# Modulation pieces moved between stages, one block-product pair reordered, and the input's fold placed behind the evictions

## The chip, the cores and the metric

The kernel runs on one core of a Trainium2 chip, in one launch. The metric is the device time in microseconds (us), the median of the runs. TensorE (PE) multiplies matrices, VectorE (DVE) and ScalarE (ACT) work elementwise, GpSimd (POOL) and SyncE (SP) here mostly issue DMAs. Each engine runs its own list of instructions in order and waits on semaphores.

## The reference, cut to what matters

One layer over 256 latent tokens (`x`) and 256 context tokens (`ctx`), with 2048 features, all in float32. The nine modulation vectors are `m = silu(c) @ ada_w + ada_b`, each of 2048 values; those for the context come from `c_ctx`.

```python
m_lat = silu(c) @ ada_w + ada_b            # 9 vectors of 2048 for the latent tokens
m_ctx = silu(c_ctx) @ ada_w + ada_b        # the context needs 0 to 4 of them
x   = x   + 0.5 * m_lat[2] * swiglu(modulate(rms_norm(x, g1),   m_lat[0], m_lat[1]), ffn1_w_in, ffn1_w_out)
ctx = ctx + 0.5 * m_ctx[2] * swiglu(modulate(rms_norm(ctx, g1), m_ctx[0], m_ctx[1]), ffn1_w_in, ffn1_w_out)
hx, hc = modulate(rms_norm(x, g2), m_lat[3], m_lat[4]), modulate(rms_norm(ctx, g2), m_ctx[3], m_ctx[4])
x = x + m_lat[5] * (concat(retention(hx, hc), mla(hx, hc)) @ mix_w_out)
x = x + 0.5 * m_lat[8] * swiglu(modulate(rms_norm(x, g3), m_lat[6], m_lat[7]), ffn2_w_in, ffn2_w_out)
return rms_norm(x, final_g)
```

`swiglu(h, w_in, w_out)` is `(silu(h @ gate) * (h @ up)) @ w_out` with 5632 inner features.

## The kernel before

**Products.** Every weight and every activation is split into a high half in fp32r and a low half (the rest), and a product is three matmuls: high by high, low by high and high by low (`three`, L1434 to L1439). A slab of weights lands in `raw`, ScalarE makes its high half `wh` with one copy, VectorE its low half `wl` with one subtraction, and TensorE starts when `wl_ready` counts the slab. Both halves have two slots, so the split of a slab can start only when the slab two before it has been used (`slab_used`). ScalarE and VectorE thus follow TensorE closely, in an order written out by hand in each engine's block.

**Stages of the first half.** 1. A start that makes modulations 0 and 1, the norm and the first three tiles of the gate and up projection. 2. The *standard slabs* (13 tiles, 26 slabs of 48 matmuls with 512 columns, to 458 us). 3. The *pair stage* (28 tiles, `FIRST_S` to `PAIRS`, 458 to 1043 us): the 2x2 block product of latent and context with gate and up halves is done in seven products of half the depth instead of eight, `P1 P5 P6 P3 P7 P2 P4` in this order, each 24 matmuls of 256 columns. They need sums of weight blocks (`w_sum` on VectorE, two accumulating DMAs on GpSimd's queue) and sums of activation blocks, made once (`form`, `last_form`, `form_hi`, `form_lo`). The last of these, the difference that P7 multiplies, overwrites `hh` and `hl`, which the standard slabs still read. P4 adds into a bank that `up_ctx` must have read after P7; `up_ctx` of a tile stands in VectorE's list behind the first low half of the next tile. 4. The *down stage* (44 steps, `STEPS`, 1043 to about 1535 us): step `(part, q, g)` multiplies group `g` of four activation tiles with quarter `q` of the output, four banks `py`, 48 matmuls with 512 columns. Parts are groups 0 to 3, 4 to 7 and 8 to 10. After the last group of a quarter the four banks are evicted: in part 0 by ScalarE (`copy_out`), in parts 1 and 2 by VectorE (`add_out`, L2418 to L2433). The next step's first matmul into a bank waits until its tile has been evicted (`y_free`). A step's iteration on ScalarE and VectorE makes the halves for the step two later (`down_high`, `down_low`). At a quarter 0, `act_high` and `act_low` also split a group of activations. 5. The *mixing stage*: squares and norm of both streams (`hl_tile`), then the slabs of the input projection, in order CQ, RQ, CKV, KR, RK, RV, RG (`S_CQ` and so on; MIX0 is the first), retention and attention. The values' banks are copied to `rv` behind every fourth RV slab. Then the second feed-forward.

**Modulation pieces.** Modulations 2 to 8 are made on VectorE, 14 rounds of 16 *pieces* (`chunk`): a piece is 128 x 1024 of `ada_w`, 512 KB, multiplied by a column of `cs` and added to a sum (`chunk_step`, L2195 to L2197). A single round ("S", modulations 5 to 8, latent only) has one sum `accl`; a double one ("D", 2 to 4) has two, `accl` and `accc`, so its piece costs two instructions. After 16 pieces the sum is reduced over the partitions: `take_turn`, `take_reduce`, `take_total`, for each sum. `STD_CHUNKS`, `S_CHUNKS` and `B_CHUNKS` say how many pieces each slab, pair and step takes. Three buffers hold pieces, and SP issues the load of a piece when the one three before it has been summed (two before it in the double rounds of the standard slabs). Before, rounds lie so: standard slabs S0 S1 D0 D1, pair stage S2 to S7, down stage D2 to D5 in steps 0 to 31.

**The input's fold.** In the down stage the input, which was overwritten, is read again and turned (`xp`, `xq`): SP loads two columns of tiles (`x_piece`), VectorE transposes 32 x 32 blocks into the two banks `two` (`turn(s)`, L2257), ScalarE copies the blocks to their places in `xq` with 16 small copies (`spread(s)`, L922), and VectorE adds (`fold(s)`, L2266). `turn(s)` waits until `spread(s-1)` has emptied the banks, `spread(s)` waits for `turn(s)` and, since `xq` is one buffer, for `fold(s-1)`; eight such rounds cover 16 tiles, from `X_STEP` on. VectorE's loop over the steps, before:

```python
for j in range(len(STEPS)):
    s = j - X_STEP
    ...
    if 1 <= s <= 8:
        fold(s - 1)
    if step_last(j) and STEPS[j][0]:
        add_out(j)
    ...
    if j + 2 < len(STEPS):
        if STEPS[j + 2][1] == 0:
            act_low(STEPS[j + 2][2])
        down_low(j + 2)
    ...
    if -1 <= s < 7:
        turn(s + 1)
```

## Time and profile before

| | |
|---|---|
| median of 3 runs | 2760.11 us (2759.91 to 2760.65) |
| profiled execution, its own time | 2760.29 us |
| its span in the profile | 2758.5 us |
| TensorE busy | 2669.7 us (97%) |
| VectorE busy | 2077.6 us (75%) |
| ScalarE busy | 1171.2 us (42%) |
| mean granted TensorE clock | 0.989 |
| mean DMA rate | 199 GB/s |

The profile is of one execution. Matmuls are pipelined, so a row of TensorE gives a duration longer than the distance from one matmul to the next. A granted clock of 1.00 is 2.4 GHz, one of 0.50 is 1.2 GHz. "A <- B" in a list of waits says that A stood idle until B had finished.

### The profile page before, as it was taken

To read this page: it belongs to the slowest core of one execution; us is meant where nothing else is said; L and a number is where in the kernel's file an instruction comes from. 1 tells how busy PE (TensorE), PEld (TensorE's weight loads), DVE (VectorE), ACT (ScalarE), POOL (GpSimd) and SP (SyncE) were. 2 spreads that over 40 slices of the span, in tenths; PEclk is the share of its full clock that TensorE was granted. 3 is DMA by queue.
4 is the path that set the end of the run, shared out by engine and by line. 5 is a ranking of instruction groups with operands and counts; after the bars stand their busy time and mean duration, and the time that the engine had idled before them with its cause. 6 is when DMAs were issued, how large, how long until landed. Compare 5 with 4: busy or idle time off the path is not lost.

```text
span 2758.5 us, 36396 instructions
## 1 busy us (share of the span) xinstructions
PE 2669.7 (97%) x14683; PEld 2323.6 (84%) x14683; DVE 2077.6 (75%) x2250; ACT 1171.2 (42%) x1290; POOL 79.7 (3%) x115
## 2 busy tenths in 40 slices
PE   6999999999999999999999899999999999999998
PEld 4778888999999998887878788888987888888887
DVE  6868788888888887778875743486677888888866
ACT  6633112443443443231146532465454545555443
POOL 0000000110111110000000000000000000000000
PEclk9999999999999999999999999999999999999999
DMA  9978776999999897566563442342445555556563
GB/s 313 298 215 264 227 226 172 264 257 254 252 262 268 234 255 253 198 208 234 183 198 115 115 121 92 123 123 89 129 142 206 195 186 198 182 199 210 173 225 122
DMA packets 426372, 550.22 MB, mean 199 GB/s; under 512 B 21762, under 2 KB 280184, under 8 KB 425464
## 3 DMA queue, kind: packets, MB, share of 16 engines
q1 hardware_dynamic: 413900, 504.64, 56.6%
q0 software_dynamic: 12080, 43.53, 7.7%
q8 instruction: 99, 1.62, 0.2%
q14 instruction: 41, 0.34, 0.0%
q10 hardware_dynamic: 252, 0.10, 0.0%
HBM read 505.22 MB, written 13.63 MB: 188 GB/s over the span
## 4 chain that ended last, share of the span: by engine, by line
PE 69%; DVE 14%; issue 5%; ACT 4%; DMA 1%; DVEq 0%; ACTq 0%; SPq 0%
PE py L1437 11%; PE py L1439 11%; PE py L1438 11%; PE pg L1437 3%; PE pg L1438 3%; PE pg L1439 3%; PE pu L1437 2%; PE pu L1438 2%; PE pu L1439 2%; DVE sraw L2755 2%; DVE wl L2744 2%; PE two L1894 2%; PE two L1895 2%; PE two L1896 2%; ACT wh L1350 1%
## 5 line engine op out<-in xcount | busy, mean ns | idle before, releaser
L2057 DVE TENSOR_TENSOR wl<-raw,wh 128x2048 fp32r<-128x2048 f32 x118 | 270.2, 2290 | 213.0 <-ACT wh L865 212.4
L865 ACT ACTIVATE wh<-raw 128x2048 fp32r<-128x2048 f32 x118 | 225.1, 1911 | 277.7 <-PE py L1439 101.7
L1010 ACT ACTIVATE wh<-raw 128x1024 fp32r<-128x1024 f32 x196 | 206.8, 1056 | 264.4 <-DVE raw L2329 207.3
L1437 PE MATMUL py<-ah,wh 128*128 128x512 f32 x704 | 275.2, 391 | 9.1 <-DVE xy L2432 6.2
L2325 DVE TENSOR_TENSOR wl<-raw,wh 128x1024 fp32r<-128x1024 f32 x196 | 238.9, 1220 | 56.0 <-ACT wh L1010 55.8
L1438 PE MATMUL py<-al,wh 128*128 128x512 f32 x704 | 274.6, 390 | 0.0
L1439 PE MATMUL py<-ah,wl 128*128 128x512 f32 x704 | 274.6, 390 | 0.0
L2197 DVE SCALAR_TENSOR_TENSOR accl<-chunk,cs,accl 128x1024 f32<-128x1024 f32 x170 | 217.8, 1281 | 53.0 <-DMA chunk<-in_ada_w 47.2
L1437 PE MATMUL py<-hh,wh 128*128 128x256 f32 (+1 forms) x656 | 200.3, 305 | 7.4 <-DVE hl L2135 5.2
L1061 ACT ACTIVATE wh<-raw 128x2048 fp32r<-128x2048 f32 x44 | 84.3, 1916 | 273.8 <-PE py L1439 273.7
L1438 PE MATMUL py<-hl,wh 128*128 128x256 f32 (+1 forms) x656 | 198.6, 303 | 0.0
L1439 PE MATMUL py<-hh,wl 128*128 128x256 f32 (+1 forms) x656 | 198.5, 303 | 0.0
L1350 ACT ACTIVATE wh<-sraw 128x2048 fp32r<-128x2048 f32 x63 | 120.9, 1919 | 169.4 <-PE two L1896 62.7
L1437 PE MATMUL pg<-hh,wh 128*128 128x256 f32 (+1 forms) x544 | 178.8, 329 | 11.6 <-DVE tv L2337 6.2
L2744 DVE TENSOR_TENSOR wl<-sraw,wh 128x2048 fp32r<-128x2048 f32 x63 | 144.1, 2288 | 57.2 <-ACT wh L1350 57.2
L2744 DVE TENSOR_TENSOR wl<-raw,wh 128x2048 fp32r<-128x2048 f32 x70 | 160.0, 2286 | 35.6 <-ACT wh L1350 35.6
L1438 PE MATMUL pg<-hl,wh 128*128 128x256 f32 (+1 forms) x544 | 178.0, 327 | 0.0
L1439 PE MATMUL pg<-hh,wl 128*128 128x256 f32 (+1 forms) x544 | 178.0, 327 | 0.0
L1437 PEld LDWEIGHTS py<-ah,wh 128*128 128x128 f32 x704 | 132.6, 188 | 39.4 <-issue 9.9
L2408 DVE TENSOR_TENSOR wl<-raw,wh 128x2048 fp32r<-128x2048 f32 x44 | 100.6, 2287 | 82.6 <-ACT wh L1061 82.6
L1437 PE MATMUL py<-fhs,wh 128*128 128x256 f32 x560 | 158.5, 283 | 0.0
L1438 PE MATMUL py<-fls,wh 128*128 128x256 f32 x560 | 158.5, 283 | 0.0
(500 smaller groups left out, 7035.0 us busy)
## 6 DMA issues: line engine op xcount, KB each, us to landing
chunk<-in_ada_w SPq DMA_DIRECT2D x182, 512.0 KB, 5.1
raw<-in_ffn_w_out SPq DMA_DIRECT2D x84, 1024.0 KB, 5.1
raw<-in_ffn_w_in SPq DMA_DIRECT2D x74, 1024.0 KB, 5.0
raw<-in_ffn_w_in SPq DMA_DIRECT2D x112, 512.0 KB, 7.3
sraw<-in_ffn_w_in SPq DMA_DIRECT2D x40, 1024.0 KB, 5.1
raw<-in_ada_w SPq DMA_DIRECT2D x64, 512.0 KB
raw<-in_mix_w_in SPq DMA_DIRECT2D x30, 1024.0 KB
raw<-raw POOLq DMA_DIRECT2D x56, 512.0 KB, 5.8
```

What stands on the lines that cost most here:

```text
L865: nc.scalar.activation(wh[:, slot % 2, :], raw[:, slot, :], ACT.Copy).then_inc(wh_ready, 1)
L1010: nc.scalar.activation(wh[:, slot, o:o + 1024], s_half(k, S_SRC[name]), ACT.Copy).then_inc(wh_ready, 1)
L1061: nc.scalar.activation(wh[:, j % 2, :], raw[:, slot, :], ACT.Copy).then_inc(wh_ready, 1)
L1350: nc.scalar.activation(whs[ring(i, name)], src, ACT.Copy).then_inc(wh_ready, 1)
L1437: mm(out_ap, w[0], xh_ap, start=first, stop=False, skip_group_check=True)
L1438: mm(out_ap, w[0], xl_ap, start=False, stop=False, skip_group_check=True)
L1439: return mm(out_ap, w[1], xh_ap, start=False, stop=last, skip_group_check=True)
L2057: tt(wl[:, slot % 2, :], raw[:, slot, :], wh[:, slot % 2, :].bitcast(F32), ALU.subtract).then_inc(wl_ready, 1)
L2197: ins = stt(a[:], chunks[PLACES[c]], cs[:, t, k:k + 1], a[:], ALU.mult, ALU.add)
L2325: tt(wl[:, slot, o:o + 1024], s_half(k, S_SRC[FORMS[pos]]), wh[:, slot, o:o + 1024].bitcast(F32), ALU.subtract).then_inc(wl_ready, 1)
L2408: tt(wl[:, j % 2, :], raw[:, b_place("w", j)[0], :], wh[:, j % 2, :].bitcast(F32), ALU.subtract).then_inc(wl_ready, 1)
L2744: tt(wls[slot], src, whs[slot].bitcast(F32), ALU.subtract).then_inc(wl_ready, 1)
```

## The change

- The single rounds S6 and S7 (modulation 8) are no longer made in the pair stage but in the mixing stage, with a sum `accm` and three buffers `chunkm` where the context stream lay. Nine slabs, from CKV+1 to RV+2, take 2, 3, 3 and six times 4 pieces. SP's `mix_chunks` issues their loads behind the slab loads. ScalarE's first copies to `rv` and TensorE's first `ret_values` get a wait for the last sum, since `rv` overwrites `accm` and `ret_values` the banks in which it is turned. `g3l`, which needs modulation 8, is computed after the attention.
- The other pieces are spread differently: in the pair stage none in the first pair, then 2 or 3 a pair; in the down stage 2 a step up to step 15, then 2, 2, 1, 1 in turn up to step 31, then 1 up to step 39.
- In the first pair of the pair stage P2 goes ahead of P7, `last_form` is cut in three parts that lie between the low halves, and `up_ctx` stands at the pair's own end.
- The input's fold and turn begin two steps sooner (`X_STEP` 30 for 32; the squares keep their steps by `N_STEP`), and `fold` stands behind `add_out` and `down_low` in the iteration. In step 28 to 31 the groups are taken in the order 6, 4, 5, 7. Three factors (`amp`) are computed at step 43 instead of 41.

```diff
@@ -48,12 +48,15 @@
 FIRST_S = EARLY + STD_PAIRS
 S_PAIRS = PAIRS - FIRST_S
 FORMS = ("P1", "P5", "P6", "P3", "P7", "P2", "P4")
+FORMS0 = ("P1", "P5", "P6", "P3", "P2", "P7", "P4")
 STD0 = ADA_SLABS
 PROD0 = STD0 + 2 * STD_PAIRS
 DOWN0 = PROD0 + len(FORMS) * S_PAIRS
 PARTS = ((0, 4), (4, 8), (8, GROUPS))
-STEPS = [(part, q, g) for part, (g0, g1) in enumerate(PARTS) for q in range(4) for g in range(g0, g1)]
-X_STEP = len(STEPS) - 12
+STEPS = [(part, q, g) for part, (g0, g1) in enumerate(PARTS) for q in range(4)
+         for g in ((6, 4, 5, 7) if (part, q) == (1, 3) else range(g0, g1))]
+X_STEP = len(STEPS) - 14
+N_STEP = len(STEPS) - 12
 MIX0 = DOWN0 + len(STEPS)
 TURNS = MIX0 // 4 - PROD0 // 4
...
@@ -420,19 +425,24 @@
             at_.append(at_[-1] + n)
         return [range(a, b) for a, b in zip(at_, at_[1:])]
 
-    ROUNDS = (("S", 0), ("S", 1), ("D", 0), ("D", 1), ("S", 2), ("S", 3), ("S", 4), ("S", 5), ("S", 6), ("S", 7),
-              ("D", 2), ("D", 3), ("D", 4), ("D", 5))
-    STD_CHUNKS = spans(8 * (3,) + 2 * (4,) + 4 * (2, 3, 2) + (2, 2) + 2 * (0,), 0)
-    S_CHUNKS = spans((3, 3) + 12 * (4, 3) + (3, 3), STD_CHUNKS[-1].stop)
-    B_CHUNKS = spans(32 * (2,) + 12 * (0,), S_CHUNKS[-1].stop)
+    ROUNDS = (("S", 0), ("S", 1), ("D", 0), ("D", 1), ("S", 2), ("S", 3), ("S", 4), ("S", 5),
+              ("D", 2), ("D", 3), ("D", 4), ("D", 5), ("S", 6), ("S", 7))
+    STD_CHUNKS = spans(10 * (3,) + (2,) + 6 * (3, 2) + (2,) + 2 * (0,), 0)
+    S_CHUNKS = spans((0,) + 5 * (2, 3, 2, 2, 3) + (2, 2), STD_CHUNKS[-1].stop)
+    B_CHUNKS = spans(16 * (2,) + 4 * (2, 2, 1, 1) + 8 * (1,) + 4 * (0,), S_CHUNKS[-1].stop)
+    M_SPLITS = (S_CKV + 1, S_KR, S_RK, S_RK + 1, S_RK + 2, S_RK + 3, S_RV, S_RV + 1, S_RV + 2)
+    M_CHUNKS = dict(zip(M_SPLITS, spans((2, 3, 3, 4, 4, 4, 4, 4, 4), B_CHUNKS[-1].stop)))
+    LATE_M = B_CHUNKS[-1].stop
     CHUNKS = KT * len(ROUNDS)
-    assert STD_CHUNKS[-1].stop == 4 * KT and S_CHUNKS[-1].stop == 10 * KT and B_CHUNKS[-1].stop == CHUNKS
+    assert STD_CHUNKS[-1].stop == 4 * KT and S_CHUNKS[-1].stop == 8 * KT and M_CHUNKS[S_RV + 2].stop == CHUNKS
     assert len(S_CHUNKS) == S_PAIRS and len(STD_CHUNKS) == 2 * STD_PAIRS and len(B_CHUNKS) == len(STEPS)
     LATE = S_CHUNKS[-1].stop
...
@@ -656,16 +672,28 @@
                 dst = raw[:, m % RAW, :] if dst is None else dst(raw[:, m % RAW, :])
                 sp.dma_start(dst, src).then_inc(raw_loaded[m % RAW], 64 // parts)
 
+            def mix_chunks(s):
+
+                if s == S_RK:
+                    sp.wait_ge(hl_ready, TILES[1])
+                    for c_ in range(LATE_M, LATE_M + 3):
+                        chunk_load(c_)
+                for c_ in M_CHUNKS.get(s - 4, ()):
+                    if c_ + 3 < CHUNKS:
+                        chunk_load(c_ + 3)
+
             def tiles(n):
                 return lambda r: r.rearrange("p (t n) -> p t n", n=n)
 
             def in_slabs(s, col, n):
                 for j in range(n):
...
@@ -1076,13 +1104,15 @@
                     nc.scalar.activation(xy[:, :, 4 * q + d, :], pair(down_banks[d][:]), ACT.Copy).then_inc(y_free, 1)
 
             def squares(s):
+                if s == 8:
+                    se.wait_ge(chunk_free, LATE_M + 1)
                 for t in range(4 * (s - 8), 4 * (s - 8) + 4):
                     square(0, t, 2 * KT + Y_F1 + t + 1)
 
             for j in range(len(STEPS)):
-                s = j - X_STEP
-                if s == 11:
-                    squares(s)
+                s, r = j - X_STEP, j - N_STEP
+                if r == 11:
+                    squares(r)
                 if step_last(j) and STEPS[j][0] == 0:
                     copy_out(j)
                 if j + 2 < len(STEPS):
@@ -1091,8 +1121,8 @@
                     down_high(j + 2)
                 else:
                     static_split(MIX0 + j + 2 - len(STEPS))
-                if 8 <= s < 11:
-                    squares(s)
+                if 8 <= r < 11:
+                    squares(r)
                 if 0 <= s < 8:
                     spread(s)
...
@@ -1168,6 +1198,8 @@
             for half in range(2):
                 for k in range(4):
                     if k == 3:
+                        if half == 0:
+                            se.wait_ge(sums_ready, (TAKEN[-1] - 1) * 5 + 1)
                         for c_ in range(4):
                             if c_ < 3:
...
@@ -1569,15 +1601,18 @@
                 pair_product(k, 2, at_x, False, True)
                 pe.wait_ge(a_p5, n + 1)
                 pair_product(k, 3, at_z, False, True)
-                pe.wait_ge(a_u2, n + 1)
                 if n == 0:
+                    pe.wait_ge(pu_free, FIRST_S + 1)
+                    pair_product(k, 4, at_y, True, True)
+                    pe.wait_ge(a_u2, n + 1)
                     pe.wait_ge(form_low, 4)
-                pair_product(k, 4, at_x, False, True)
-                if n >= 2:
-                    pe.wait_ge(a_c11, n - 1)
-                elif n == 0:
-                    pe.wait_ge(pu_free, FIRST_S + 1)
-                pair_product(k, 5, at_y, True, True)
+                    pair_product(k, 5, at_x, False, True)
+                else:
+                    pe.wait_ge(a_u2, n + 1)
+                    pair_product(k, 4, at_x, False, True)
+                    if n >= 2:
+                        pe.wait_ge(a_c11, n - 1)
+                    pair_product(k, 5, at_y, True, True)
                 pe.wait_ge(a_v, n + 1)
                 pair_product(k, 6, at_x, False, True)
...
@@ -2291,11 +2330,15 @@
                 else:
                     tt(fls[k][:], flt[k][:], fhs[k][:].bitcast(F32), ALU.subtract).then_inc(form_low, 1)
 
-            def last_form():
+            def last_form(step_):
                 a = slice(0, HALF)
-                tt(h21[0][:], hh[:, 0, a, :].bitcast(F32), hh[:, 1, a, :].bitcast(F32), ALU.subtract)
-                link(tt(h21[1][:], hl[:, 0, a, :].bitcast(F32), hl[:, 1, a, :].bitcast(F32), ALU.subtract))
-                tt(h21[1][:], h21[0][:], h21[1][:], ALU.add).then_inc(form_sum, 1)
+                if step_ == 0:
+                    ve.wait_ge(slab_used, PROD0)
+                    tt(h21[0][:], hh[:, 0, a, :].bitcast(F32), hh[:, 1, a, :].bitcast(F32), ALU.subtract)
+                elif step_ == 1:
+                    link(tt(h21[1][:], hl[:, 0, a, :].bitcast(F32), hl[:, 1, a, :].bitcast(F32), ALU.subtract))
+                else:
+                    tt(h21[1][:], h21[0][:], h21[1][:], ALU.add).then_inc(form_sum, 1)
 
             def std_mult(k):
...
@@ -2354,22 +2397,23 @@
             for k in range(FIRST_S, PAIRS):
                 span = S_CHUNKS[k - FIRST_S]
                 half_low(k, 0)
-                if k > FIRST_S:
+                if k > FIRST_S + 1:
                     up_ctx(k - 1)
                 w_sum(k, 0, 1)
                 half_low(k, 1)
                 w_sum(k, 0, 2)
                 if k == FIRST_S:
+                    last_form(0)
+                    half_low(k, 2)
+                    last_form(1)
+                    half_low(k, 3)
                     std_mult(k - 1)
-                    half_low(k, 2)
-                    half_low(k, 3)
-                    last_form()
+                    last_form(2)
                     half_low(k, 4)
+                    half_low(k, 5)
                     form_lo(3)
-                    half_low(k, 5)
                     half_low(k, 6)
-                    for c_ in span:
-                        chunk_step(c_)
+                    up_ctx(k)
                 else:
                     gate_lat(k - 1)
                     for c_ in span[:-3]:
@@ -2394,6 +2438,8 @@
                             take_reduce(c_, 0)
                         if n and ends_round(c_ - 1):
                             take_total(c_ - 1, 0)
+                    for n in range(len(span), 3):
+                        half_low(k, 4 + n)
                     if ends_round(span[-1]):
                         take_total(span[-1], 0)
                 up_lat(k)
...
@@ -2438,37 +2484,36 @@
                     square_add(0, t)
 
             for j in range(len(STEPS)):
-                s = j - X_STEP
+                s, r = j - X_STEP, j - N_STEP
                 if s == 0:
                     ve.wait_ge(ada_summed, TAKEN[4])
                     link(ts(g1l[:], ml[:, 2 * KT:3 * KT], 0.5, None, ALU.mult))
                     link(ts(g1c[:], mc[:, 2 * KT:3 * KT], 0.5, None, ALU.mult))
-                if s == 9:
-                    ve.wait_ge(ada_summed, 20)
+                if s == 13:
+                    ve.wait_ge(ada_summed, TAKEN[-3])
                     amp(a2l, 4, ml, V_N2)
                     amp(a2c, 4, mc, V_N2)
                     amp(a3l, 7, ml, V_N3)
-                if 1 <= s <= 8:
-                    fold(s - 1)
                 if step_last(j) and STEPS[j][0]:
                     add_out(j)
-                if s == 11:
-                    square_adds(s)
+                if r == 11:
+                    square_adds(r)
                 if j + 2 < len(STEPS):
                     if STEPS[j + 2][1] == 0:
                         act_low(STEPS[j + 2][2])
                     down_low(j + 2)
                 else:
                     static_split(MIX0 + j + 2 - len(STEPS))
-                if 8 <= s < 11:
-                    square_adds(s)
+                if 1 <= s <= 8:
+                    fold(s - 1)
+                if 8 <= r < 11:
+                    square_adds(r)
                 if j:
                     late_takes(B_CHUNKS[j - 1])
                 chunk_span(B_CHUNKS[j])
                 if -1 <= s < 7:
                     turn(s + 1)
-            ve.wait_ge(ada_summed, 20)
-            link(ts(g3l[:], ml[:, 8 * KT:9 * KT], 0.5, None, ALU.mult))
+            ve.wait_ge(ada_summed, TAKEN[-3])
             roots(0, 0)
             for t in range(KT):
                 hl_tile(0, 0, xl, a2l, ml[:, 3 * KT:4 * KT], t)
...
@@ -2501,18 +2546,25 @@
             latent_norm(0)
             rotate(0, rq[:, 0, :], 0)
             rotate(1, rq[:, 1, :], 0)
+            chunk_span(M_CHUNKS[S_CKV + 1])
             static_split(MIX0 + S_KR)
             rotate(2, rq[:, 2, :], 0)
+            chunk_span(M_CHUNKS[S_KR])
             static_split(MIX0 + S_RK)
             rotate(3, rq[:, 3, :], 0)
+            chunk_span(M_CHUNKS[S_RK])
             for j in range(4):
                 static_split(MIX0 + S_RK + j + 1)
+                chunk_span(M_CHUNKS[S_RK + j + 1])
             latent_norm(1)
             rotate(4, rk[:, 0, 0:LAT], 0)
             static_split(MIX0 + S_RV + 1)
+            chunk_span(M_CHUNKS[S_RV + 1])
             rotate(5, rk[:, 1, 0:LAT], 0)
             for q in range(3):
                 static_split(MIX0 + S_RV + q + 2)
+                if q == 0:
+                    chunk_span(M_CHUNKS[S_RV + 2])
                 if q < 2:
                     rotate(6 + q, rk[:, 2 + q, 0:LAT], 0)
...
@@ -2695,6 +2747,8 @@
             out_low(HEADS - 1)
             out_add(HEADS - 1, py[3])
             static_split(MIX0 + S_OUTM + 1)
+            ve.wait_ge(ada_summed, TAKEN[-1])
+            link(ts(g3l[:], ml[:, 8 * KT:9 * KT], 0.5, None, ALU.mult))
             for t in range(KT):
                 ins = ts(diag[:, t, :], eyes[:, 0, :], g3l[:, t:t + 1], None, ALU.mult)
```

## Rows read from the trace of the kernel before

**Rows 1.** Windows, whole core (us on each engine, clock, DMA share, GB/s)
```profile
458.00:1043.60 585.60, 571.43 (x4705) 569.72 (x4705) 488.94 (x543) 250.11 (x338) 63.42 (x84) 0.99 0.93 249
1043.60:1540.00 496.40, 483.62 (x2116) 397.80 (x2116) 365.24 (x406) 171.94 (x234) 1.10 (x2) 1.00 0.58 194
1605.00:1731.00 126.00, 126.00 (x553) 103.53 (x552) 43.37 (x46) 29.66 (x25) 0.00 (x0) 1.00 0.30 93
475.10:481.30 6.20, 6.16 (x29) 6.19 (x30) 5.99 (x7) 0.00 (x0) 0.00 (x0) 0.50 0.35 103
1433.30:1437.10 3.80, 3.77 (x10) 3.01 (x11) 3.80 (x7) 3.69 (x10) 0.00 (x0) 0.55 0.07 21
937.20:942.10 4.90, 4.87 (x23) 4.87 (x24) 3.78 (x4) 1.33 (x2) 0.87 (x1) 0.50 0.49 99
```

**Rows 2.** Waits of TensorE, 458 to 1043 us (total, times, longest)
```profile
PE pg L1437 <- DVE tv L2337: 6.2, 4, 4.1
PE pg L1437 <- DVE hl L2290: 5.4, 1, 5.4
PE py L1437 <- DVE tv L2337: 2.2, 2, 1.2
```

**Rows 3.** Waits of TensorE, 1043 to 1540 us
```profile
PE py L1437 <- DVE xy L2432: 6.2, 2, 4.9
...
PE py L1437 <- DVE xy L2428: 1.7, 1, 1.7
```

**Rows 4.** Timeline, VectorE, first pair (start, duration, what, idle before)
```profile
459.34 1.22 DVE L2329 TENSOR_TENSOR raw<-raw 128x1024 f32<-128x1024 f32 x1
...
463.96 2.28 DVE L2296 TENSOR_TENSOR h21h<-hh 128x2048 f32<-128x2048 f32 x1
...
472.75 2.29 DVE L2290 TENSOR_TENSOR hl<-h21l,hh 128x2048 fp32r<-128x2048 f32 x1 [0.84 <-ACT hh L983]
```

**Rows 5.** Timeline, ScalarE, first pair
```profile
470.81 1.91 ACT L983 ACTIVATE hh<-h21l 128x2048 fp32r<-128x2048 f32 x1 [3.55 <-DVE h21l L2298]
```

**Rows 6.** Timeline, VectorE, a pair from 565 to 584 us
```profile
565.18 0.41 DVE L2337 TENSOR_TENSOR tv<-tv,pg 128x256 f32<-128x256 f32 x1
...
583.29 0.42 DVE L2337 TENSOR_TENSOR tv<-tv,py 128x256 f32<-128x256 f32 x1
```

**Rows 7.** Timeline, VectorE, down stage, 1404 to 1436 us
```profile
1405.44 0.73 DVE L2207 STREAM_TRANSPOSE pg<-accl 128x512 f32<-128x512 f32 x1
...
1410.54 0.68 DVE L2207 STREAM_TRANSPOSE pu<-accc 128x512 f32<-128x512 f32 x1
...
1429.54 1.32 DVE L2257 STREAM_TRANSPOSE two<-xp 128x512 f32<-128x512 f32 x2 [4.21 <-ACT xq L922]
1430.77 0.44 DVE L2266 SCALAR_TENSOR_TENSOR xy<-xy,g1l,xq 128x256 f32<-128x256 f32 x1
...
1432.32 0.48 DVE L2432 SCALAR_TENSOR_TENSOR xy<-py,g1l,xy 128x256 f32<-128x256 f32 x1
...
1435.46 2.28 DVE L2408 TENSOR_TENSOR wl<-raw,wh 128x2048 fp32r<-128x2048 f32 x1
```

**Rows 8.** Timeline, ScalarE, down stage
```profile
1423.23 6.18 ACT L922 ACTIVATE xq<-two 32x256 f32<-32x256 f32 x16 [2.65 <-DVE xy L2266]
1429.43 1.91 ACT L1061 ACTIVATE wh<-raw 128x2048 fp32r<-128x2048 f32 x1
```

**Rows 9.** Groups by line: one piece into one sum
```profile
L2197 DVE SCALAR_TENSOR_TENSOR accl<-chunk,cs,accl 128x1024 f32<-128x1024 f32 x170 | 217.8, 1281 | 53.0 <-DMA chunk<-in_ada_w 47.2
```

**Rows 10.** Timeline, VectorE, mixing stage
```profile
1674.09 3.35 DVE L2495 RECIPROCAL rms<-rms 128x512 f32<-128x512 f32 x1
...
1683.30 2.29 DVE L2057 TENSOR_TENSOR wl<-raw,wh 128x2048 fp32r<-128x2048 f32 x1 [3.17 <-ACT wh L865]
```

**Rows 11.** DMA issues, 1300 to 1540 us (count, size, us to landing)
```profile
chunk<-in_ada_w SPq DMA_DIRECT2D x17, 512.0 KB, 3.9
```

**Rows 12.** DMA issues, 740 to 1040 us
```profile
chunk<-in_ada_w SPq DMA_DIRECT2D x33, 512.0 KB, 7.7
```

More of the change, by code:

```diff
@@ L172, in build @@
     accc = at("accc", [P, CH], F32, o_e + 12 * KB)
+    accm = at("accm", [P, CH], F32, o_xc)
+    chunkm = [at(f"chunkm{k}", [P, CH], F32, o_xc + (4 + 4 * k) * KB) for k in range(3)]
     xp = at("xp", [P, 2, 4, P], F32, o_hh)
@@ L405, in build @@
     TILES = (KT, 3 * KT)
-    chunks = [chunk[:, 0, :], chunk[:, 1, :], accc[:], chunk3[:]]
+    chunks = [chunk[:, 0, :], chunk[:, 1, :], accc[:], chunk3[:]] + [t[:] for t in chunkm]
     XBANKS = py + pgu
@@ L435, in chunk_place @@
         kind, _ = ROUNDS[c // KT]
+        if c >= LATE_M:
+            return 4 + (c - LATE_M) % 3
         if kind == "S":
@@ L443, in build @@
     PLACES = [chunk_place(c) for c in range(CHUNKS)]
-    SIGNAL = [p % 3 if p < 3 else 2 for p in PLACES]
+    SIGNAL = [2 if p == 3 else p % 4 for p in PLACES]
     LOADS = [sum(SIGNAL[k] == SIGNAL[c] for k in range(c + 1)) for c in range(CHUNKS)]
@@ L447, in build, with forms, prod_of @@
     TAKEN = [sum(1 if kind == "S" else 2 for kind, _ in ROUNDS[:r]) for r in range(len(ROUNDS) + 1)]
+    def forms(k):
+        return FORMS0 if k == FIRST_S else FORMS
+    def prod_of(k, name):
+        return prod(k, forms(k).index(name))
     def prod(k, pos):
@@ L562, in chunks_ahead @@
                 for c_ in span:
-                    while loaded_to[0] < CHUNKS and (BEFORE[loaded_to[0]] is None or BEFORE[loaded_to[0]] <= c_):
+                    while loaded_to[0] < LATE_M and (BEFORE[loaded_to[0]] is None or BEFORE[loaded_to[0]] <= c_):
                         if PLACES[loaded_to[0]] == 3 and c_ < LATE + 2:
@@ L610, in _ @@
                 span = S_CHUNKS[k - FIRST_S]
-                for n, (pos, r) in enumerate(((3, 2), (4, 1), (5, 3), (6, 0))):
+                for n, (pos, r) in enumerate(((3, 2), (5, 1), (6, 3), (6, 0)) if k == FIRST_S else ((3, 2), (4, 1), (5, 3), (6, 0))):
                     if k + 2 < PAIRS:
@@ L1539, in pair_product @@
                 slot, o = half_slot(n)
-                name = FORMS[pos]
+                name = forms(k)[pos]
                 for t in range(HALF):
@@ L1707, in ret_values @@
                 pe.wait_ge(rp_ready, h + 1)
+                if h == 0:
+                    pe.wait_ge(sums_ready, (TAKEN[-1] - 1) * 5 + 2)
                 if h == 4:
@@ L2205, in take_turn @@
                 ve.wait_ge(chunk_free, c + 2)
-                for h, b in enumerate(pab if c < LATE else pgu):
-                    ins = nc.vector.transpose(b[:], (accl, accc)[k][:, h * 512:(h + 1) * 512])
+                if c == LATE_M + KT - 1:
+                    ve.wait_ge(proj_free, QT + 2)
+                for h, b in enumerate(pgu if LATE <= c < LATE_M else pab):
+                    ins = nc.vector.transpose(b[:], (accm if c >= LATE_M else (accl, accc)[k])[:, h * 512:(h + 1) * 512])
                 ins.then_inc(sums_ready, 1)
@@ L2212, in take_reduce @@
                 ve.wait_ge(sums_ready, v * 5 + 1)
-                for h, b in enumerate(pab if c < LATE else pgu):
+                for h, b in enumerate(pgu if LATE <= c < LATE_M else pab):
                     ins = nc.vector.tensor_reduce(s32[:, 0, 16 * h:16 * h + 16], b[:].rearrange("p (c q) -> p c q", q=32), AX.X, ALU.add)
```

16 lines of the change are left out of this document (9 added, 7 removed).

## The prediction, made before the change was built

> **What bounds the kernel.** The windows by stage come first [rows 1]: the reader is to see that TensorE is busy for 571.4 of 585.6 us in the pair stage and for 483.6 of 496.4 in the down stage, while no other engine is above 84%. So only TensorE's own waits, and what its clock loses behind them, can be won or lost. VectorE does the low halves, the modulation pieces and all the small sums, in one order written out by hand; the waits of TensorE say that it is VectorE, late, that TensorE waits for. In the pair stage the waits sum to 8.4 us for `up_ctx` (six) and 5.4 for the last form [rows 2]; in the down stage to 6.2 us for the evictions in `add_out` of the last part (two, one of 4.9) and 1.7 for those of the middle part [rows 3]. The same windows give the clock: after the 5.4 us wait it was granted 0.50 (1.2 GHz) for 6.2 us, after the 4.1 us wait 0.50 for 4.9 us, after the 4.9 us wait 0.55 for 3.8 us [rows 1]. At half clock half of the time is lost: 3.1, 2.4 and 1.7 us. All that the change can give back is thus 13.8 + 5.5 in the pair stage and 7.9 + 1.7 in the down stage.
>
> **Pair stage, first pair.** TensorE starts the first product at 458.0 and needs 2.88 us for each. P7 was due at 469.6, but its low half `form_lo(3)` ended at 475.0 [rows 4]. In the new order the difference (`last_form`) is cut in three and begins behind the two `w_sum`, at 460.5 [rows 4]. VectorE then runs, with 1.14 us for a half-slab of 1.22 that overlaps its neighbour and 2.2 for a form of 2.28: form 0 to 462.7, low of P6 463.9, form 1 466.1, low of P3 467.3, `std_mult` and its flag 0.8 to 468.1, form 2 470.3, low of P2 471.5, low of P7 472.6. ScalarE's high half takes 1.91 [rows 5], from 470.3 to 472.3, so `form_lo(3)` ends at 474.9. TensorE: P6 waits 0.1, P3 0.5, P2 (now ahead of P7) 1.2, P7 0.5. P4 now follows P7 directly, and `up_ctx`, 0.41 [rows 6], stands between them with nothing to cover it: 0.7 with the two hand-overs. Sum 3.0 in waits under 1.3 us, instead of 5.4 + 3.1 = 8.5: **-5.5**. Bounds: nothing better than 0 left (-8.5), and -3 if one of the five waits doubles and the clock falls.
>
> **Pair stage, the rest.** Thirty-two pieces of 1.28 us [rows 9] leave it: 2 or 3 a pair instead of 3 or 4. From one `up_ctx` to the next, with three pieces, VectorE's chain is 565.2 to 583.3, 18.1 us, of which it waits little [rows 6]; a pair is 7 x 2.88 = 20.2. A single round's take is `take_turn` to `take_total`, 1405.4 to about 1410.0, near 4.5 of the 5.8 that a double one needs [rows 7]. Then 18.1 + 4.5 = 22.6 is late by 2.4, and P2, 2.88, covers it; with a fourth piece and a wait for its load it was not covered. The load waits (47.2 us for `chunk` in the whole kernel [rows 9]) go too, since the load of each piece is issued 16 us ahead where a fourth piece had a landing of 7.7 in the way [rows 12]. So 6.2 + 2.2 + 2.4 = 10.8 and 0.4 at the start of the down stage go: **-11.2**; bounds -12 and -6 (two rounds in three-piece pairs still late by as much as before).
>
> **Standard slabs.** Two pieces more of the double kind fall in three-piece steps: 3 x 2.45 + 2.2 + 0.8 = 10.4 of a step of 10.9, and the first double round ends as the first of three, 5.8 us more. A low half may be 6.6 us late before TensorE sees it; I find 3.2 us left at the worst step. 0, bound +1.
>
> **Down stage: the fold behind the evictions.** This is the decisive part. A step is 483.6 / 44, some 10.9 us. `turn` 1.24, `spread` 6.18, `fold` 1.6, split 1.91 on ScalarE and low half 2.2 on VectorE [rows 7, 8]. Before, `fold(s-1)` stands at the head of the iteration: turn, fold, spread are a ring of 9.1 us, and it fits in a step. In the new text `fold(s-1)` stands behind `down_low`, `spread(s)` on ScalarE waits for that fold, `turn(s+1)` at the end of the same VectorE iteration waits for that spread, and the next split stands behind the spread on ScalarE. The ring is 1.6 + 6.2 + 1.9 + 2.2, with hand-overs 12.1: longer than a step. And VectorE sits in `turn` while the next eviction is due. With 0 = end of step 29: spread(0) ends at 19.1 and turn(1) at 20.4; step 31's `add_out`, `act_low(9)` and the low half of step 33 end at 27.2, fold(0) 28.9, spread(1) 35.2; behind it `act_high(10)` (1.9, as the split) and the split end at 39.0, `act_low(10)` and the low half at 41.6, fold(1) 43.3, spread(2) 49.5, low half 53.7, fold(2) 55.4, spread(3) 61.6, turn(4) 62.9, first tile of `add_out(34)` 63.8. Step 34 ends at 54.4, and step 35 needs that tile: a wait of **9.1 us** where 4.9 was. The same sum on the order of before, with its own takes, gives 5.1 and 1.2 us for the two waits that were 4.9 and 1.3 [rows 3], so I trust it. The clock falls as after the 5.4 us wait: 2.8 more. From there three rings up to `add_out(37)`: turn(7) ends some 3.7 after step 37, the first tile 0.9 later: 4.6, and 2.0 for the clock. Last, the final double take now ends round 39 of the down stage, one iteration ahead of `add_out(40)`: 2.1 + 2.2 + 2.4 + 5.7 = 12.4 after the end of step 39, plus 0.9 for the first tile, against 10.9: 2.4, and up to 1.5 for the clock. `add_out(19)` has one piece less ahead of it (1.7 becomes 0.3); `add_out(27)` gets a take ahead of it, 0.6. New sum 9.1 + 2.8 + 4.6 + 2.0 + 2.4 + 1.5 + 0.3 + 0.6 = 23.3; old 7.9 + 1.7 = 9.6: **+13.7**. Bounds: +3 if no lag builds up (a wait of 3.3 is then left at each of the two evictions, from 13.3 + 0.9 against 10.9), +18 if the clock stays down longer. Moving the two steps sooner does not help; it puts the ring onto `act_high(9)` and `act_high(10)`. The new order of groups in steps 28 to 31 only frees the buffer for `xp`: 0. SP's `x_piece` loads, two of 128 KB for each, go two steps sooner with it; they wait for `turn` as before, and the slab loads behind them in SP's queue are due three steps later: 0.
>
> **Mixing stage.** Thirty-two pieces (41 us) and two takes (9 us) go where VectorE has 83 us of 126 free and the DMA queues are at 0.30 [rows 1]. The three buffers cover three pieces of a span; the fourth is issued when the first is summed, so with a landing of 3.9 [rows 11] it waits 1.5. Followed slab by slab, the low half due at the start of RV+3 is ready 2 us early: `latent_norm(1)` from 1674.1 and `rotate(4)` push the low of 1683.3 [rows 10] to 1688.8, four pieces and `rotate(5)` the next to 1698.7, four pieces, the take and `rotate(6)` the last to 1713.1, due 1715.2. Each us more in landing adds 3 to it; with a slab load of 1 MB issued just ahead I take 5.1: **+1.0**, bounds 0 and +6. The Trainium skill, DMA: Bandwidth & Descriptors, Anatomy of one DMA, gives a fixed 2.0 us plus bytes over 436 GB/s; an estimate from it is 3.2 us for a piece, and with that this term would be 0. No landing here is under 3.9, so the trace does not agree. Three waits are added. ScalarE's at the first `rv` copies and TensorE's at the first `ret_values` want the last take, which has its turn at 1706.5, before the fourth value slab, behind which the copies stand, even starts (1715.2): 0; late, they would hold the value banks, and so TensorE. SP's `chunk_load` holds the next slab load until a piece is summed, and that slab is due two slabs later: 0. `squares` wants the pieces of step 39, summed one step before. `g3l` moved behind the mixing saves 0.2 ahead of the first norm tile.
>
> **Sum.** -5.5 - 11.2 + 0 + 13.7 + 1.0 - 0.2 = -2.2. The profiled execution took 2760.3 us (span 2758.5), 0.2 above the median of 2760.1: **2758 us**.
>
> **Rivals.**
> *The lag does not build up, or VectorE is back in time (faster)*. For it: 3.3 us is all that the ring forces at each eviction, and ScalarE is only 35% busy [rows 1]. Against it: every wait in the ring stands in the code. With +3 for +13.7 the sum is -12.9, 2747; with both evictions in time 4.8 us of the new sum are left, -4.8 for +13.7, and it is 2740.
> *Late pieces in mixing (slower)*: landing as in the pair stage, 7.7 [rows 12] for 3.9. The last three spans then are each 3.8 later, 11.4 in all, less 2.1 slack: 9.3 us and a fall of the clock, 2.4. It decides from a landing of about 6 us on. For it: each load follows a slab load on the same queue; against it: 93 GB/s there against 249. 2758 + 11 = 2769.
> *The pair stage gains little (slower)*: the takes still hold `up_ctx`, and only 6 of 11.2 come back, with the first pair at -3: 2766.
> *A ring worse than summed (slower)*: +18 for +13.7: 2762, within my range.
>
> **How the numbers follow.** My forecast 0.66, first rival 0.17, second 0.09, third 0.08. Around 2758 the unknown terms (first pair 2, ring 4, mixing 3) spread by about 5 either way: 2752 to 2764. Eight in ten reaches to the near end of the first rival and to the second: 2742 to 2769. About 0.2%, 5.5 us, is what a measurement of this kernel can tell from no change: 2754.6 to 2765.6. Faster: the first rival and a quarter of my own case, 0.33. Slower: most of the other two and a little of mine, 0.18. Same: 0.49.
>
> **What would show it.** Right: no wait above 1.3 us between 458 and 480 us, and no half-clock stretch in the pair stage; no wait for `tv` there; a wait for `xy` of about 9 us at the fourth step of the last part, a second of 4 to 5 three steps on, a third of 2 to 3 at the last quarter, each behind a `turn` that waited for `xq`; no wait above 1 us in mixing. Wrong: VectorE's evictions starting as soon as the banks are done in steps 34 and 37; a wait for `wl` in the value slabs; or waits for `tv` still there.

## The result, and the profile after

The changed kernel takes 2768.32 us, median of 18 runs (2763.84 to 2771.58); the kernel before, run beside it, 2759.68 us (18 runs, 2755.64 to 2763.81). The ratio is 1.0032, 95% interval 1.0025 to 1.0038: **slower by 0.32%, 8.6 us**, where 2758 and most likely no change was forecast. The time lies within the range of 2742 to 2769.

The profiled execution took 2771.58 us, span 2769.8. It is the longest of the 18, 3.3 us above the median, so the profile shows 11.3 us more than that of before where the medians show 8.6.

Where the time went is seen from four instructions of TensorE that both kernels have, read from the timeline: the first product of the down stage, the first sum over `ssum` behind it, the first gate product of the mixing stage's last third, and TensorE's last instruction.

| TensorE starts, us | before | after | stage longer by | forecast |
|---|---|---|---|---|
| first product of the down stage | 1043.60 | 1029.64 | -14.0 (standard slabs and pairs) | -16.7 |
| first sum over `ssum` | 1538.89 | 1538.16 | +13.2 (down) | +13.7 |
| first gate product, mixing | 1769.99 | 1780.88 | +11.6 (mixing) | +0.8 |
| last instruction | 2749.09 | 2760.38 | +0.4 | 0 |

The down stage came as forecast. The standard slabs and pairs gave back 2.7 us less than forecast, and the mixing stage is most of the miss: 11.6 for 0.8. The windows of the changed kernel show the same, with the columns of [rows 1]: the pair stage, the down stage, the mixing stage, then five stretches at low clock.

```profile
458.00:1029.60 571.60, 566.75 (x4707) 565.02 (x4706) 451.23 (x489) 249.41 (x337) 64.08 (x84) 1.00 0.89 227
1029.60:1538.00 508.40, 486.32 (x2114) 400.02 (x2112) 363.34 (x404) 170.76 (x233) 1.10 (x2) 0.98 0.57 189
1605.00:1740.00 135.00, 127.88 (x538) 103.33 (x538) 87.94 (x102) 28.39 (x25) 0.00 (x0) 0.96 0.63 206
1417.80:1428.00 10.20, 5.67 (x13) 4.46 (x14) 7.88 (x15) 4.04 (x7) 0.00 (x0) 0.51 0.32 98
1462.10:1465.60 3.50, 2.71 (x7) 2.16 (x8) 3.50 (x9) 0.39 (x1) 0.00 (x0) 0.54 0.00 0
1499.70:1503.10 3.40, 3.39 (x9) 2.65 (x10) 3.40 (x7) 1.92 (x7) 0.00 (x0) 0.53 0.01 2
1694.20:1698.50 4.30, 2.78 (x6) 1.77 (x7) 4.16 (x4) 0.00 (x0) 0.00 (x0) 0.53 0.11 15
1725.00:1728.40 3.40, 3.40 (x10) 2.58 (x10) 3.30 (x5) 0.00 (x0) 0.00 (x0) 0.53 0.71 220
```

The pair stage has no stretch at half clock any more, and 4.9 us of TensorE's idle time where [rows 1] had 14.2. The mixing stage had TensorE busy for all of its 126.0 us before; now 7.1 of 135 are idle, and its clock falls twice. TensorE's waits, 458 to 1029 us, then 1029 to 1540 us, then 1605 to 1740 us, each line with total, times and longest:

```profile
PE pg L1469 <- DVE wl L2368: 2.3, 2, 1.4
PE pu L1469 <- DVE wl L2368: 1.0, 1, 1.0
PE py L1469 <- DVE wl L2368: 0.7, 2, 0.4
PE pg L1469 <- DVE tv L2380: 0.6, 1, 0.6
...
PE py L1469 <- DVE xy L2478: 16.9, 3, 9.4
...
PE py L1469 <- DVE xy L2474: 0.7, 1, 0.7
PE py L1469 <- DVE wl L2454: 0.7, 2, 0.4
...
PE pg L1676 <- DVE rk L2534: 4.4, 2, 3.5
PE py L1710 <- DVE wl L2094: 2.7, 2, 1.6
```

The last two lines had no counterpart in the kernel before, which waited for nothing there. The first bout, TensorE's timeline at the second value slab (RV+1):

```profile
1694.62 1.22 PE L1676 MATMUL pg<-rk,eyes 128*128 128x256 f32 x2 [3.46 <-DVE rk L2534]
1696.94 0.80 PE L1710 MATMUL py<-wh,hh 128*128 128x512 f32 x1 [1.10 <-DVE wl L2094]
```

TensorE waits for `rk`, the result of `rotate(4)`, because the product with the swap matrix (L1676) stands in its order just ahead of the slab, and right behind it for the slab's low half. On VectorE the two also stand one behind the other, the low half last, so it is the low half that decides when the slab starts. VectorE comes to both late. Its timeline there:

```profile
1678.98 4.06 DVE L2234 SCALAR_TENSOR_TENSOR accm<-chunkm,cs,accm 128x1024 f32<-128x1024 f32 x3
1687.31 1.29 DVE L2234 SCALAR_TENSOR_TENSOR accm<-chunkm,cs,accm 128x1024 f32<-128x1024 f32 x1 [4.27 <-DMA chunkm<-in_ada_w]
1688.51 3.35 DVE L2540 RECIPROCAL rms<-rms 128x512 f32<-128x512 f32 x1
...
1694.14 0.42 DVE L2534 TENSOR_TENSOR rk<-rk,rope_t 128x256 f32<-128x256 f32 x1
1694.60 2.29 DVE L2094 TENSOR_TENSOR wl<-raw,wh 128x2048 fp32r<-128x2048 f32 x1
```

The bracket is what matters: three pieces of the span follow each other, then VectorE sits for 4.27 us until the fourth piece has landed, and only then come the latent norm (1674.09 in [rows 10], 1688.51 now), the rotation and the low half (1683.30 there, 1694.60 now). VectorE's waits over the whole stage, 1605 to 1730 us:

```profile
DVE accm L2234 <- DMA chunkm<-in_ada_w: 24.0, 7, 4.9
```

### The profile page after: what moved, and what is told of

Same layout as the page of the kernel before. It is cut to its first block, busy times and chain, and to the rows that moved or that the text cites. A ratio compares the mean times of both kernels' runs of the same rounds, so it can differ in the third digit from the quotient of the medians.

```text
span 2769.8 us, 36399 instructions
## 1 busy us (share of the span) xinstructions
PE 2673.2 (97%) x14683; PEld 2323.4 (84%) x14683; DVE 2084.5 (75%) x2250; ACT 1169.9 (42%) x1290; POOL 79.8 (3%) x115
## 4 chain that ended last, share of the span: by engine, by line
PE 65%; DVE 15%; issue 6%; ACT 5%; DMA 3%; DVEq 0%; ACTq 0%; SPq 0%
PE py L1469 10%; PE py L1470 10%; PE py L1471 10%; PE pg L1469 3%; PE pg L1470 3%; PE pg L1471 3%; DVE sraw L2809 2%; PE pu L1469 2%; DVE wl L2798 2%; PE pu L1470 2%; PE pu L1471 2%; DMA chunkm<-in_ada_w 2%; PE two L1931 2%; DVE wl L2094 2%; PE two L1933 2%
## 5 line engine op out<-in xcount | busy, mean ns | idle before, releaser
L1469 PE MATMUL py<-ah,wh 128*128 128x512 f32 x704 | 276.9, 393 | 18.3 <-DVE xy L2478 16.9
L2234 DVE SCALAR_TENSOR_TENSOR accl<-chunk,cs,accl 128x1024 f32<-128x1024 f32 x150 | 192.2, 1281 | 26.9 <-DMA chunk<-in_ada_w 22.0
```

What stands on the lines that cost most here:

```text
L1469: mm(out_ap, w[0], xh_ap, start=first, stop=False, skip_group_check=True)
L2234: ins = stt(a[:], chunks[PLACES[c]], cs[:, t, k:k + 1], a[:], ALU.mult, ALU.add)
```

## The experiments

Each is timed beside the kernel before on the same chip (2759.83 us beside e1 to e4, 2759.88 beside e5 to e8). The changed kernel was not timed again beside them; its 2768.3 is the median above, taken beside a kernel before of 2759.68.

### A fourth buffer, or the load issued earlier: mixing stage

**e1_buf4**, the fourth buffer:

```diff
-chunkm = [... for k in range(3)]                 # 4 KB each behind accm
+chunkm = [... for k in range(3)] + [one more, at o_a + 12 KB]
-return 4 + (c - LATE_M) % 3
+return 4 + (c - LATE_M) % 4
-    chunk_load(c_ + 3)
+    chunk_load(c_ + 4)
```

> The changed kernel with a fourth buffer for the mixing pieces, so that all four pieces of a span are loaded one span ahead. Theory (the fourth piece of a span waits for a load that could only be issued when the first was summed): VectorE's waits for chunkm fall from 4.1 to 4.9 us each in the last spans to under 1.5, TensorE's waits in the mixing stage (3.6, 2.2, 1.1 and 2.1 us, with some 3.2 us lost to the clock) nearly go, and the kernel is 8 to 11 us faster than the changed one: 2757 to 2760 us. Rival (VectorE has too much work in front of its rotation and latent norm, loads or not): the waits for chunkm go but rotate(4) still ends late, TensorE still waits 2 us or more there, and at most 4 us come back.

Measured: 2757.08 us (11 runs, 2755.22 to 2759.07), ratio to before 0.9991 (0.9982 to 1.0): 11.2 us less than the changed kernel. VectorE waits for no `chunkm` at all, TensorE for nothing above 0.5 us in the stage. The rival falls: 50 us of added VectorE work fit into the stage, if their data are there.

**e4_first**, three buffers, another order on SP's queue:

```diff
+                    mix_first(s + j)      # chunk_load for the 4th piece of the span
                     mix_slab(s + j, ...)  # 1 MB
-                    mix_chunks(s + j)     # all loads of the span
+                    mix_chunks(s + j)     # all but the first
```

> The changed kernel with the load for the fourth piece of each mixing span issued ahead of that step's 1 MB slab load on SP's queue, the others behind it as they were. Theory (the slab load just ahead lengthens the landing): the landing of those pieces falls from about 5.7 to 4 us, VectorE's waits for chunkm from 4.1 to 4.9 to about 3, and 3 to 6 us come back: 2762 to 2765 us. Rival (the landing is as long without the slab load ahead, or the slab load becomes late in turn): no change or slower, 2767 to 2772 us.

Measured: 2756.81 us (11 runs, 2754.38 to 2759.45), ratio 0.9988 (0.9979 to 0.9997): 11.5 us less than the changed kernel, twice what I expected. The reason is in single loads, seen on their own in the DMA issues (count, size, us to landing). In the changed kernel, issued at 1698.1 behind the slab load of 1696.9, and at 1640.8 and 1680.3:

```profile
chunkm<-in_ada_w SPq DMA_DIRECT2D x1, 512.0 KB, 5.5
...
chunkm<-in_ada_w SPq DMA_DIRECT2D x1, 512.0 KB, 6.8
...
chunkm<-in_ada_w SPq DMA_DIRECT2D x1, 512.0 KB, 7.0
```

In this kernel, issued at 1688.2 and 1698.0, each ahead of the slab load:

```profile
chunkm<-in_ada_w SPq DMA_DIRECT2D x1, 512.0 KB, 3.7
...
chunkm<-in_ada_w SPq DMA_DIRECT2D x1, 512.0 KB, 3.6
```

Over the six spans of four pieces, the load of the fourth piece landed in 6.8, 7.6, 6.8, 7.0, 5.5 and 5.5 us in the changed kernel, and in 5.3, 3.9, 3.6, 3.6, 3.7 and 3.6 here. In both it is issued when the first piece of its span has been summed, so only what stands ahead of it differs. My expectation had judged by the median of all 32 loads, 5.7, and that hardly moved (5.5). VectorE's waits:

```profile
DVE accm L2241 <- DMA chunkm<-in_ada_w: 9.1, 9, 1.5
```

Nine waits of about 1 us remain, and TensorE sees none of them: the stage is busy throughout, with the clock never below full.

```profile
1605.00:1730.00 125.00, 125.00 (x548) 102.69 (x547) 90.25 (x105) 29.66 (x25) 0.00 (x0) 1.00 0.65 222
```

The Trainium skill, DMA: Bandwidth & Descriptors, section Queues, rings and completion order, says that each DMA engine consumes the descriptors of SP's queue in ring order; that a load therefore lands later by what the bytes ahead of it take is my conclusion, and the trace agrees with it (5.5 behind a slab, 3.6 ahead of it). At the 436 GB/s that the same page of the Trainium skill gives in Anatomy of one DMA, there for loads issued from GpSimd, 1 MB ahead is 2.4 us, an estimate; the six pairs of loads show 1.5 to 3.7.

### The fold back ahead of the evictions: down stage

**e2_fold**, the two steps sooner kept:

```diff
+                if 1 <= s <= 8:
+                    fold(s - 1)
                 if step_last(j) and STEPS[j][0]:
                     add_out(j)
 ...
                 down_low(j + 2)
-                if 1 <= s <= 8:
-                    fold(s - 1)
```

> The changed kernel with the fold of the input put back ahead of the evictions and the low half, still two steps sooner than before. Theory (the ring turn, fold, spread, split, low half is longer than a step): the waits of 9.4 and 4.9 us at the evictions of the last part, and the half clock behind them, become two or three of about 1.2 us; the wait of 2.5 us at the last quarter, which is the late take's, stays; the recurrence that gave the 9.1 us says 13.7 us less in the down stage: 2753 to 2757 us. Rival (the pieces and takes of the down stage are what is late, not the place of the fold): the big waits stay above 4 us and less than 6 us come back, above 2762.

Measured: 2752.3 us (9 runs, 2749.62 to 2754.85), ratio 0.9973 (0.9963 to 0.9983): 16.0 us less than the changed kernel, and 0.7 below the range that I expected. TensorE's waits from 1029 to 1518 us, where the changed kernel had 16.9 and 0.7:

```profile
PE py L1469 <- DVE xy L2478: 5.1, 3, 2.5
PE py L1469 <- DVE xy L2474: 1.7, 2, 1.0
```

The 9.4 and 4.9 us are gone, 1.3 and 1.3 stand in their place, and the 2.5 us of the late take stays. In the profiles the down stage is 16.2 us shorter (TensorE starts 1027.87 and 1520.20): 10.8 of it are waits, and the rest is the clock, which is never down there, not even behind the 2.5 us wait that is left. These are the shortest of this kernel's 9 runs and the longest of the changed kernel's 18, 22.0 us apart (the mixing stage gives 3.8 of them), so the 16.2 hold some luck. The rival falls: what comes back in the medians is nearly three times its bound of 6. The ring can be read off the timelines of the changed kernel: VectorE's first, then ScalarE's.

```profile
1412.06 0.48 DVE L2305 SCALAR_TENSOR_TENSOR xy<-xy,g1l,xq 128x256 f32<-128x256 f32 x1
...
1420.12 1.32 DVE L2296 STREAM_TRANSPOSE two<-xp 128x512 f32<-128x512 f32 x2 [4.00 <-ACT xq L950]
1421.35 0.44 DVE L2478 SCALAR_TENSOR_TENSOR xy<-py,g1l,xy 128x256 f32<-128x256 f32 x1
```
```profile
1401.70 6.18 ACT L950 ACTIVATE xq<-two 32x256 f32<-32x256 f32 x16 [4.40 <-DVE xy L2305]
1407.90 1.92 ACT L1089 ACTIVATE wh<-raw 128x2048 fp32r<-128x2048 f32 x1
1413.82 6.17 ACT L950 ACTIVATE xq<-two 32x256 f32<-32x256 f32 x16 [4.00 <-DVE xy L2305]
```

From one spread to the next it is 12.12 us (the prediction had 12.1) where a step is 10.9; each engine sits 4.0 us waiting for the other within it, and the first tile of the eviction (1421.35) comes after the `turn` that waited.

### The standard slabs, and the first pair

**e3_std**:

```diff
-STD_CHUNKS = spans(10 * (3,) + (2,) + 6 * (3, 2) + (2,) + 2 * (0,), 0)
+STD_CHUNKS = spans(8 * (3,) + 2 * (4,) + 4 * (2, 3, 2) + (2, 2) + 2 * (0,), 0)
```

> The changed kernel with the spans of the standard slabs as they were in the kernel before (four pieces in two steps, two and three in the others). Theory (VectorE comes 3.3 us late out of the standard slabs, and that lateness is what the first pair waits for beyond the forecast): the waits of the first pair, 5.9 us in all, fall to 2.5 to 3.5, and the kernel is 2.5 to 3.5 us faster than the changed one: 2765 to 2766 us. Rival (the new order of the first pair costs this by itself): the waits stay near 5.9 and the time at 2768.

Measured: 2765.86 us (11 runs, 2763.67 to 2769.69), ratio 1.0024 (1.0015 to 1.0033): 2.5 us less. VectorE's first low half of the pair stage starts at 454.80 (458.07 in the changed kernel, 454.71 before), and the waits of the first pair are 0.2, 0.5, 1.1, 0.3 and 0.8 us, 3.0 in all for 5.9, against 3.0 forecast (0.1, 0.5, 1.2, 0.5, 0.7). A wait is here the distance between two matmuls beyond the usual 0.12, so the hand-over is in it; the profile's list, idle time alone, has 2.0. The intervals of the two ratios overlap, so the 2.5 us rest on the trace as much as on the times. Where the 3.3 us came from is seen in VectorE's waits from 300 to 458 us, in the changed kernel and then in this one:

```profile
DVE accl L2234 <- DMA chunk<-in_ada_w: 15.5, 5, 5.5
```
```profile
DVE accl L2234 <- DMA chunk<-in_ada_w: 10.8, 8, 3.2
```

**e7_firstonly**, the kernel before with nothing but the first pair's order:

```diff
-                    std_mult(k - 1); half_low(k, 2); half_low(k, 3); last_form()
-                    half_low(k, 4); form_lo(3); half_low(k, 5); half_low(k, 6)
+                    last_form(0); half_low(k, 2); last_form(1); half_low(k, 3)
+                    std_mult(k - 1); last_form(2); half_low(k, 4); half_low(k, 5)
+                    form_lo(3); half_low(k, 6); up_ctx(k)
                     for c_ in span:          # three pieces, as before
                         chunk_step(c_)
```

> The kernel before with the new order of the first pair alone (its three pieces stay, behind up_ctx). Theory (the first pair gives back what was forecast where VectorE isn't late from the standard slabs): the wait of 5.4 us and 3.1 us of half clock become waits of 2.7 to 3.5 us in all, none above 1.3 us: 5 to 6 us less than before, 2753.5 to 2755. Rival (the three pieces and up_ctx behind it make the next pair late, so that the gain is waited for again): 2757 or more.

Measured: 2758.85 us (11 runs, 2755.28 to 2762.23), ratio 0.9998 (0.9989 to 1.0007): no change, the rival's case. The 5.4 us wait and the clock's fall are gone, but waits of the first pair and then of the second, behind the three pieces, take their place; TensorE's waits from 458 to 500 us:

```profile
PE py L1444 <- DVE wl L2339: 2.5, 3, 1.9
PE pu L1444 <- DVE wl L2339: 1.0, 1, 1.0
PE py L1444 <- ACT p1a L1024: 0.9, 1, 0.9
PE py L1444 <- ACT tv L1024: 0.8, 1, 0.8
PE pg L1444 <- DVE tv L2351: 0.6, 1, 0.6
```

The fifth product of the second pair starts at 498.18 us, in the kernel before at 498.07, so nothing has come back by then. In e3_std, with the same order and no pieces in the first pair, it starts at 493.47. The new order thus pays only because the change also leaves the first pair without pieces. That VectorE's work bounds the two pairs together is my reading of it; two of the eight waits, 1.7 us, are for ScalarE.

### Together, and further

**e5_three** joins the edits of e2, e4 and e3.

> The changed kernel with three repairs together: the fold ahead of the evictions, the first load of each mixing span ahead of the slab load, the standard slabs' spans of the kernel before. Alone they gave 16.0, 11.5 and 2.5 us. Theory (three separate lateness terms of VectorE, each in its own stage): they add up, 30 us less than the changed kernel, 2736 to 2741 us, and what is left against the kernel before, some 21 us less, is the gain of the first pair and the pair stage (forecast 5.5 and 11.2) and of smaller terms. Rival (what is won early is waited for later, since the stages share VectorE's order and the loads): 2743 us or more.

Measured: 2740.48 us (5 runs, 2739.02 to 2742.15), ratio 0.9927 (0.9913 to 0.9941): 27.8 us less than the changed kernel, where the three alone sum to 30.0. They add up but for 2 us, which is no more than the runs of one kernel spread. In the profiled executions the waits of the down stage are those of e2_fold, but it is 1.5 us longer, since the clock here falls behind the 2.5 us wait. TensorE starts at 1026.78, 1520.64 and 1751.47: the standard slabs and pairs are 16.8 us shorter than before (forecast 16.7), the down stage 1.4, the mixing stage 0.3.

**e8_pairs3** moves one of the two mixing rounds back to the pair stage:

```diff
-S_CHUNKS = spans((0,) + 5 * (2, 3, 2, 2, 3) + (2, 2), ...)
+S_CHUNKS = spans((0,) + 26 * (3,) + (2,), ...)
-M_CHUNKS = ... spans((2, 3, 3, 4, 4, 4, 4, 4, 4), ...)
+M_CHUNKS = ... spans((0,) + 8 * (2,), ...)
```

> As the kernel with three repairs, but five rounds in the pair stage instead of four (three pieces in every pair) and one round in the mixing stage instead of two (two pieces a span). Theory (P2 covers a take and three pieces; a fourth piece was what made up_ctx late): no wait for tv above 0.5 us in the pair stage, the mixing stage without any wait for a piece, and the time within 2 us of the three repairs: 2736 to 2741 us. Rival (three pieces with a take in every fifth or sixth pair already make up_ctx late): waits for tv of 1 to 2 us at each of the five takes, and 4 to 8 us more.

Measured: 2740.85 us (5 runs, 2739.49 to 2742.88), ratio 0.9931 (0.9918 to 0.9945), as e5_three. TensorE's waits in the pair stage are those of the first pair and nothing else:

```profile
PE pu L1476 <- DVE wl L2375: 1.0, 1, 1.0
PE pg L1476 <- DVE tv L2387: 0.6, 1, 0.6
PE py L1476 <- DVE wl L2375: 0.4, 1, 0.4
```

The 0.6 for `tv` is a little above the 0.5 expected, and it is the first pair's. So a take and three pieces a pair are covered, in each of the five rounds, and it makes no difference whether the mixing stage takes one round or two.

**e6_inner** puts the fold inside the eviction, and moves the last double take:

```diff
                 for d in range(4):
                     k = 4 * q + d
+                    if d == 1 and 1 <= j - X_STEP <= 8:
+                        fold(j - X_STEP - 1)
-B_CHUNKS = spans(... + 8 * (1,) + 4 * (0,), ...)
+B_CHUNKS = spans(... + (2,) + 6 * (1,) + 5 * (0,), ...)
```

> As the kernel with three repairs, and the fold behind the first of an eviction's four tiles instead of ahead of them, and the last double round of the down stage ended one step sooner (two pieces in step 32), so that its take no longer stands ahead of the eviction of step 40. Theory (the waits left at the evictions are the fold or the take ahead of the first tile): the three waits of 1.1 to 1.4 us and the one of 2.7 at the last quarter fall below 0.7 each, and it is 4 to 7 us faster than the three repairs alone: 2731 to 2735 us. Rival (the evictions wait for the banks or the tile's other inputs, or the take is in the way where it stands now): less than 2 us.

Measured: 2733.13 us (4 runs, 2731.39 to 2734.26), ratio 0.9902 (0.9887 to 0.9917): 7.4 us less than e5_three and 26.8 less than the kernel before, the fastest here. Of the evictions' waits from 1029 to 1518 us two short ones are left:

```profile
PE py L1476 <- DVE xy L2483: 0.8, 1, 0.8
...
PE py L1476 <- DVE xy L2487: 0.3, 1, 0.3
```

## Why the prediction was right, and where it failed

**The failed step is the mixing stage's term**, "with a slab load of 1 MB issued just ahead I take 5.1: +1.0". It measured 11.6 in the profile and 11.2 to 11.5 by the two repairs. The mechanism was named, the fourth piece that waits for its own landing; the size was wrong. The landing of the deciding loads was 5.5 to 7.6 us, not 5.1, so six waits of 2.7 to 4.9 us came, 22.9 in all, where 1.5 to 2.7 each was counted. And the waits were not followed from the first span on: the sum starts at 1674.1, the time of the kernel before, as if the spans ahead had cost VectorE nothing. With such a wait a span takes VectorE 11.7 us, from its low half at 1676.78 to the norm at 1688.51, and a slab takes TensorE 11.4, so lateness is not made good; with the short waits of e4_first the same stretch takes 8.4 (1670.21 to 1678.60). VectorE came to the pieces ahead of the norm at 1678.98, 4.9 late, and they took 9.5 us with their wait of 4.3. The low half of RV+1 was to be ready at 1688.8 and was at 1696.9, due at about 1691; that of RV+3, forecast for 1713.1, was ready at 1724.7. Behind each the clock falls (0.53 from 1694.2 and from 1725.0). The bound of +6 was too low for the same reason. The second rival, late pieces in mixing at 2769, is what happened, and its "decides from a landing of about 6 us on" fits; it was given 0.09. The sentence "No landing here is under 3.9" is a misreading: 3.9 is the median of those loads, their shortest is 3.4, 0.2 above the estimate of 3.2 that it was set against.

**The first pair**, -5.5: right in its waits where VectorE arrives in time (3.0 us in e3_std, 3.0 forecast), 2.9 us of waits too low in the changed kernel. The step that failed is the standard slabs' "0, bound +1": the three-piece steps come 3.3 us late by a load wait of 5.5 us. The landings were left out of that sum, the same omission as in mixing. That e7_firstonly gains nothing also shows that the 5.5 needed two edits, the order and a first pair without pieces; the forecast's working names only the order.

**The pair stage**, -11.2: right. No wait behind the first pair, no fall of the clock; with the standard slabs mended, both terms together are 16.8 for 16.7.

**The down stage**, +13.7: right in its parts. Waits of 9.4, 4.9 and 2.5 us were forecast as 9.1, 4.6 and 2.4; the first two stand behind a `turn` that waited for `xq`, the third behind the late take, as its sum had it (its list of signs says a `turn` for all three). The stage is 13.2 longer. The half clock behind them cost 2.8, 1.4 and 1.7 us (from the first matmul behind the wait until they are 0.23 us apart again, less 0.23 for each), forecast as 2.8, 2.0 and 1.5. Undoing the fold alone gives 16.0, more than the 13.2, since with the two steps sooner the stage comes out 3.0 shorter than before (492.3 for 495.3 us): waits of 0.7, 1.0, 1.3, 1.3 and 2.5 and no fall of the clock, where [rows 3] had 7.9 and [rows 1] the clock's fall, 1.7. That the clock stayed up behind the 2.5 us wait cannot be counted on: in e5_three, with the same waits, it fell there, and the stage was 1.4 shorter than before.

**The first rival**, that the lag does not build up, is refuted by the 9.4 us and by e2_fold. **The third**, little gained in the pair stage, is refuted. The three added waits (ScalarE's, TensorE's, SP's) cost nothing that shows: with the loads repaired TensorE is busy for all of 125 us there. The 0.2 for `g3l` is too small to be told from the spread between executions.

What stays open: the five waits of the standard slabs' loads were not taken apart one by one, so which of the spans made the 5.5 us wait is argued from the trace and only their joint effect is shown.

## What to carry to other kernels

Work moved to an engine that is half idle costs what its data cost: ask for each piece when its load can be issued at the earliest, and what stands ahead of it on the queue, before adding up busy times. For a load that somebody waits for, take its own landing behind what is queued there, never the median of its group. Start the sum at the first span of moved work: where a span with its wait takes longer than the step it has to fit into, the lateness adds up from span to span. And a gain ahead of a busy engine may be waited for again a little later.
